# Moving the SBUF buffers of a two-block transformer kernel so that weights and inputs lie 320 bytes apart modulo 512

## The chip, the cores and the metric

The kernel runs on one core of a Trainium2 chip, as one program. The metric is the device time of one execution in microseconds (us). Three runs of the kernel before took 2302.91 to 2307.69 us, with a median of 2307.36 us.

## What is computed

The reference is two blocks of two layers each, on 256 tokens of width 1024, in float32. A layer of the first block is: half a SwiGLU feed-forward of hidden width 2816, an attention mixer (a projection to 2840 columns, three kinds of sparse attention in 8 heads and a further 8 heads of block attention, an output product), and another half feed-forward. A layer of the second block is: a projection, an RWKV-7 recurrence in matrix form, a retention branch and a gated spatial branch, whose results are multiplied by branch weights, weighed by gates and sent through an output product; then a feed-forward of width 2816 with a convolution of three taps.

```
x = x + 0.5 * swiglu(rms_norm(x, norm_ffn1[l]), w_ffn1_gate[l], w_ffn1_up[l], w_ffn1_down[l])
x = x + hybrid_mixer(rms_norm(x, norm_mix[l]), w_in[l], ...)
x = x + 0.5 * swiglu(rms_norm(x, norm_ffn2[l]), ...)
...
x = x + jnp.sum(gates * proj, axis=2) @ w_out[l]
x = x + conv_ffn(rmsnorm(x, norm2_g[l]), ffn_w_up[l], ffn_conv_w[l], ffn_conv_b[l], ffn_w_down[l])
```

## The kernel before

Every large matrix product is made three times, to come near float32 with a faster type: each operand is split into a high and a low part, and `matmul3` (L85 to L91) issues high by high (L89), high by low (L90) and low by high (L91) into the same PSUM bank. Each of the three loads its own 128x128 stationary operand. Weights arrive in SBUF by DMA from the SP queue, ScalarE writes the high part (L341, L351, L638, L1779), VectorE the low part (L417, L435, L645, L1784).

The tokens stand transposed in `hT` (high and low part, 8 blocks of 128 rows by 256 tokens), written once in each phase from four PSUM banks.

**Feed-forward** (`ffn_phase`, four times in the first block, and with `conv` twice in the second). The hidden width is cut into 11 chunks. For chunk i, `hidden(i, slot)` makes the gate and the up product: 2 halves, 2 matrices, 8 blocks, 3 products, so 96 products with a weight block stationary and 256 columns of `hT` moving. Then `down` makes 24 products of the chunk before, with the activation stationary and 512 columns of the down weights moving. Weights of even chunks stand in slot 0 and those of odd chunks in slot 1; the two slots are separate buffers (`mem.parts[slot]`). Chunks 0, 1 and 2 are written out, chunks 3 to 8 are a loop, 9 and 10 are written out again. PE's order is hidden(0), hidden(1), down(0), hidden(2), down(1), hidden(3), down(2) and so on; down uses the slot of its own chunk.

**Mixer and projection** (`nsa_phase`, `rw_project_phase`). Units of 256 weight columns pass through a ring of three buffers. Most jobs are 24 products with weights stationary and 256 columns of `hT` moving; some are turned round, with tokens stationary and 256 (in one unit 280) columns of weights moving. In the mixer, most jobs run in halves of 12 products between steps of the attention.

**Scan and mix** (`scan_mix_phase`). Pieces of 1024 weight columns pass through another ring of three. A gate piece is 24 products with `normed_T_parts` moving, a branch piece 24 with `branches_T` or `rw_T_parts` moving, and an output piece has `merged_parts` stationary and 512 columns of weights moving. Pieces stand between the small products of the recurrence on PE.

At the start of a phase PE turns the normalised tokens, and `keep_clock` (L148) issues products of the identity with itself so that PE doesn't stand still.

All buffers are put at addresses by hand. `first_map` and `second_map` give each a column (4 bytes) from the map's base: the first map holds the buffers of the first block, the second those of the second block. Buffers of different times share memory. The order of work on the engines, the semaphores and the DMA queues do not depend on these columns.

Of the kernel before, what the change touches and what calls it, by code (L numbers as in the profile page):

```python
# [12 lines left out]
P = 128  # L13
D = 1024
KT = D // P
S = 256
# [7 lines left out]
DH = 64  # L24
# [4 lines left out]
Q_COLS = NH * DH  # L29
# [5 lines left out]
CMP_LEN, CMP_STRIDE, CMP_HID = 32, 16, 256  # L35
N_CMP = (S - CMP_LEN) // CMP_STRIDE + 1
CJ = CMP_LEN * DH // P
# [39 lines left out]
F32R = mybir.dt.float32r  # L77
# [164 lines left out]
def blocks(first, *shape):  # L242

    width = KT * FF_W
    if not shape:
        return first
    step = width * int(np.prod(shape[1:]))
    return [blocks(first + n * step, *shape[1:]) for n in range(shape[0])]
# [366 lines left out]
UNIT = KT * 2 * P  # L615
# [49 lines left out]
N_WORK = 3 * NT * 4 * NH + 3 * NT * P + NT * NH  # L665
W_UNIT = KT * (2 * P + GATE_COLS)


def first_map(nc, c):

    def at(name, col, shape, dtype=F32):
        return nc.alloc_sbuf_tensor_at(name, shape, dtype, offset=FIRST_BASE + 4 * col)

    c.ffn = FfnMemory(at, "ffn", dict(hT=0, act=4096, arrived_down=6144, arrived=(blocks(9168, 2), blocks(23152, 2)),
                                      parts=(blocks(13264, 2, 2), blocks(27248, 2, 2)), down_parts=blocks(35440, 2, 2)))
    c.hT_parts = at("mixer_T_parts", 0, [P, 2, KT, S], F32R)
    c.wc1 = at("w_cmp1", 4096, [P, 2, CJ, CMP_HID])
    c.attention = at("attention", 4096, [P, 10 * S + N_WORK])
    c.branch_rows = at("branch_rows", 4096 + 10 * S + N_WORK, [P, 3, Q_COLS])
    c.wc2 = at("w_cmp2", 12288, [P, 2, 2, 2, DH])  # L680
    c.pos = at("pos", 12800, [P, 2, CJ])
    c.raw = at("raw", 12832, [P, N_TURNED, S])
    c.rot = at("rot", 17440, [P, N_ROT, S])
    c.vtok = at("v_tokens", 21024, [P, NT, 2 * P + Q_COLS])
    c.gates = at("gates", 22560, [P, NT, GATE_COLS])
    c.kc = at("k_cmp", 22608, [P, GROUPS, 16])
    c.vc = at("v_cmp_by_head", 22640, [P, NH, DH])
    widths = (UNIT, UNIT, W_UNIT)
    c.units_arrived = [at(f"mixer_arrived{n}", col, [P, w]) for n, (col, w) in enumerate(zip((23152, 25200, 43632), widths))]
    c.units_parts = [[at(f"mixer_parts{n}_{lo}", col + lo * w, [P, w], F32R)[:] for lo in range(2)] for n, (col, w) in enumerate(zip((27248, 31344, 35440), widths))]  # L690
    c.cos_part = c.work[:, 0:2 * S].rearrange("p (a n) -> p a n", a=2)

    c.kcols = c.h[:].rearrange("p t d -> p (t d)")[:, 0:2 * GROUPS * CJ * N_CMP].rearrange(
        "p (v g j n) -> p v g j n", v=2, g=GROUPS, j=CJ)
    hid_w = 2 * 2 * GROUPS * 16
    c.hid = c.work[:, 2 * S:2 * S + hid_w].rearrange("p (v f g n) -> p v f g n", v=2, f=2, g=GROUPS)
    c.hid_v = c.work[:, 2 * S + hid_w:2 * S + hid_w + 2 * NH * 16].rearrange("p (f g r n) -> p f g r n", f=2, g=GROUPS, r=REP)
# [796 lines left out]
def first_block(nc, c, c2, a, start, tables2, out):  # L1494
# [8 lines left out]
    def follow(before, ph):  # L1503
        before.nxt, ph.prev = ph, before

    first_map(nc, c)
    ffn1 = ffn(0, "ffn1")
    ffn1.start = start
# [13 lines left out]
    follow(nsa2, ffn4)  # L1522
    ffn4.count_first()
    second_map(nc, c2)
    halves = [HalfUnits(c2, c2.half_sems, l) for l in range(DEPTH)]

# [127 lines left out]
UNITS = 2 * NH  # L1654
# [44 lines left out]
def second_map(nc, c):  # L1699

    def at(name, col, shape, dtype=F32):
        return nc.alloc_sbuf_tensor_at(name, shape, dtype, offset=SECOND_BASE + 4 * col)

    c.hT_parts = at("normed_T_parts", 0, [P, 2, KT, S], F32R)
    c.vecs = at("vectors", 4096, [P, 40])
    c.mu, c.w0, c.a0, c.k_k, c.k_a, c.r_k = (c.vecs[:, a:b] for a, b in
                                             ((0, 14), (14, 18), (18, 22), (22, 26), (26, 30), (30, 34)))
    c.low_rank = at("low_rank", 4136, [P, 2 * RW_W])
    c.vt = at("rw_v_tokens", 5160, [P, NT, RW_W])
    c.ret_rot = at("ret_rot", 6184, [P, 4, S])  # L1710
    c.ret_v = at("ret_v", 7208, [P, NT, RET_H * RET_V])
    c.ret_g = at("ret_g", 8232, [P, NT, RET_H * RET_V])
    c.st = at("row_stats", 9256, [P, 64])
    kept = at("rw_kept", 9320, [P, 4, PAIRS * S])
    c.gt = at("rw_g_tokens", 13416, [P, NT, RW_W])
    c.bonus = at("rw_bonus", 14440, [P, NT, NH])
    c.rw_small = at("rw_small", 14456, [P, 3, PAIRS, NT])

    LOCAL = 14480
    local = at("rw_local", LOCAL, [P, 8, PAIRS * S])  # L1720
    c.rw = [local[:, n] for n in range(6)] + [kept[:, n] for n in range(4)] + [local[:, n] for n in (6, 7)]
    c.kr = kept[:, 2:4].rearrange("p a n -> p (a n)").rearrange("p (j c n) -> p j c n", j=PAIRS, c=NT)
    c.ret_raw = at("ret_raw", LOCAL + 8192, [P, 4, S])
    c.thin = at("thin", LOCAL + 9224, [P, 2, S])
    c.units_arrived = [at(f"rw_project_arrived{n}", col, [P, UNIT])[:] for n, col in enumerate((36504, 38552, 40600))]
    c.units_parts = [[at(f"rw_project_parts{n}_{lo}", col, [P, UNIT], F32R)[:] for lo, col in enumerate(cols)]
                     for n, cols in enumerate(((24216, 26264), (28312, 34456), (30360, 32408)))]

    c.first_arrived = [at(f"first_project_arrived{n}", col, [P, UNIT])[:] for n, col in enumerate((28312, 40600, 36504))]
    c.first_parts = [[at(f"first_project_parts{n}_{lo}", col, [P, UNIT], F32R)[:] for lo, col in enumerate(cols)]  # L1730
                     for n, cols in enumerate(((24216, 26264), (38552, 34456), (30360, 32408)))]

    c.pairs_of = at("pairs", LOCAL, [P, UNITS, 3 * P])[:]
    c.z_t = at("inverse_T", LOCAL + 6144, [P, UNITS, P])[:]
    c.inner = at("inner", LOCAL + 8192, [P, 2, 512])
    c.rhs0 = at("rw_rhs", LOCAL + 9216, [P, RW_W])
    c.z = at("inverse", 37528, [P, UNITS, P])[:]
    c.low = at("level_rows", 39576, [P, 2, 512])
    c.a_rows = at("a_rows", 34456, [P, UNITS, P])[:]
    c.y_parts = at("branches_T", 26264, [P, 2, 2, 4, S], F32R)  # L1740
    c.half_arrived = [at(f"mix_arrived{n}", col, [P, HALF_UNIT])[:] for n, col in enumerate((40600, 41624, 36504))]
    c.half_parts = [at(f"mix_parts{n}", col, [P, 2, HALF_UNIT], F32R) for n, col in enumerate((30360, 32408, 24216))]
    c.y_rw_parts = at("rw_T_parts", 7208, [P, 2, 4, S], F32R)
    c.merged_parts = at("merged_parts", LOCAL, [P, 2, KT, S], F32R)
    c.conv_ffn = FfnMemory(at, "conv_ffn", dict(hT=18576, act=40600, arrived=(blocks(8192, 2), blocks(26264, 2)), arrived_down=12288,
                                                parts=(blocks(0, 2, 2), ((36504, 38552), (24216, 34456))),
                                                down_parts=((14480, 16528), (30360, 32408)), taps=22672))


R_, K_, V_, A_, LW, KK, BH, KH, KR, KR2, E1, E2 = range(12)  # L1750
# [390 lines left out]
HALF_UNIT = D  # L2141
# [856 lines left out]
```

## Time and profile before

| | |
|---|---|
| median of 3 runs | 2307.36 us |
| the profiled execution | 2309.51 us, its span 2307.7 us |
| PE busy | 2216.4 us, 96% of the span |
| VectorE, ScalarE busy | 1411.9 us, 1005.6 us |
| mean granted clock | 0.981 |
| DMA | 349.08 MB, 41.6% of 16 engines' time |

The profile records the start and a modelled end of each matmul. Matmuls are pipelined, so the duration of one (279 ns for those of 256 columns in the feed-forward) is longer than the step from one start to the next. What a product costs in a row of products is that step: the length of a stretch by the number of products that start in it. In the view of windows, a stretch that begins with the first product of a row and ends with the start of what follows shows its length in the first figure; the count behind it also holds the one to three products of before and after that reach over its edges.

### The profile page before, as it was taken

Reading aid. Unit: us, or ns where it says so; the run is one execution under the profiler, and the core shown is the slowest. Engines: PE = TensorE matmul, PEld = TensorE weight load, DVE = VectorE, ACT = ScalarE, POOL = GpSimd, SP = SyncE. Lnnn points to the kernel's source line nnn. Section 1 sums busy time; section 2 is a strip of 40 time slices with the busy share of each in tenths; the row PEclk is TensorE's granted clock in tenths of the full one; section 3 lists DMA queues with packets and bytes.
Section 4 is the critical chain, followed back from the end, with each engine's and each line's share of the span. In section 5 each row is a group of like instructions: output and inputs, shape, how many; then the busy total and the mean of one; then the engine's idle time right before and its main releaser. Section 6 shows DMA issues by size and latency. Waiting matters only on the chain. (4 is left out here: it accounts for less than half of the span.)

```text
span 2307.7 us, 39093 instructions
## 1 busy us (share of the span) xinstructions
PE 2216.4 (96%) x16210; PEld 2062.3 (89%) x16210; DVE 1411.9 (61%) x2091; ACT 1005.6 (44%) x1409; POOL 18.8 (1%) x18
## 2 busy tenths in 40 slices
PE   7999999999999999999999899899999989989998
PEld 7999977999999997899889799889988979988997
DVE  6545456654654645655476666577677666657775
ACT  5434355433533445633355333364545433336453
POOL 0000000000000000000000100000000010000000
PEclk9999999999999999999999899999999989999999
DMA  8445322553454522354443233365434322336551
GB/s 317 176 157 196 119 101 92 219 216 148 193 214 159 198 84 83 146 219 165 171 148 119 65 96 95 93 254 196 179 114 160 119 76 85 101 96 252 201 182 46
DMA packets 79579, 349.08 MB, mean 151 GB/s; under 512 B 21200, under 2 KB 30544, under 8 KB 45520
## 3 DMA queue, kind: packets, MB, share of 16 engines
q1 hardware_dynamic: 79440, 347.07, 41.6%
q8 instruction: 106, 1.74, 0.3%
q14 instruction: 33, 0.27, 0.0%
HBM read 345.99 MB, written 1.05 MB: 150 GB/s over the span
## 5 line engine op out<-in xcount | busy, mean ns | idle before, releaser
L89 PE MATMUL bank<-ffn_hT_split,n_split_gate_up 128*128 128x256 f32 x1408 | 392.3, 279 | 2.8 <-DVE ffn_hT_split L192 2.7
L90 PE MATMUL bank<-ffn_hT_split,n_split_gate_up 128*128 128x256 f32 x1408 | 392.2, 279 | 0.0
L91 PE MATMUL bank<-ffn_hT_split,n_split_gate_up 128*128 128x256 f32 x1408 | 391.7, 278 | 0.0
L89 PEld LDWEIGHTS bank<-ffn_hT_split,n_split_gate_up 128*128 128x128 f32 x1408 | 265.2, 188 | 4.8 <-issue 3.1
L90 PEld LDWEIGHTS bank<-ffn_hT_split,n_split_gate_up 128*128 128x128 f32 x1408 | 265.1, 188 | 1.5
L91 PEld LDWEIGHTS bank<-ffn_hT_split,n_split_gate_up 128*128 128x128 f32 x1408 | 265.1, 188 | 0.0
L1784 DVE TENSOR_TENSOR mix_parts<-mix_arrived,mix_parts 128x1024 fp32r<-128x1024 f32 x88 | 107.4, 1224 | 137.4 <-ACT mix_parts L1779 137.1
L356 ACT ACTIVATE work<-bank 128x256 f32<-128x256 f32 x88 | 33.3, 383 | 315.6 <-PE bank L91 315.5
L454 DVE TENSOR_TENSOR work<-bank,work 128x256 f32<-128x256 f32 x88 | 37.3, 423 | 197.7 <-ACT work L356 197.7
L435 DVE TENSOR_TENSOR ffn_split_down<-ffn_arrived_down,ffn_split_down 128x2048 fp32r<-128x2048 f32 x44 | 100.8, 2291 | 85.4 <-ACT ffn_split_down L351 85.4
L417 DVE TENSOR_TENSOR n_split_gate_up<-arrived_gate_up,n_split_gate_up 128x2048 fp32r<-128x2048 f32 x64 | 144.7, 2288 | 12.7 <-ACT n_split_gate_up L341 12.7
L1779 ACT ACTIVATE mix_parts<-mix_arrived 128x1024 fp32r<-128x1024 f32 x88 | 92.8, 1056 | 131.5 <-PE bank L91 129.1
L89 PE MATMUL bank<-ffn_split_down,ffn_act_split 128*128 128x512 f32 x352 | 139.0, 395 | 0.0
L91 PE MATMUL bank<-ffn_split_down,ffn_act_split 128*128 128x512 f32 x352 | 138.9, 395 | 0.0
L90 PE MATMUL bank<-ffn_split_down,ffn_act_split 128*128 128x512 f32 x352 | 138.9, 395 | 0.0
L351 ACT ACTIVATE ffn_split_down<-ffn_arrived_down 128x2048 fp32r<-128x2048 f32 x44 | 84.4, 1917 | 112.2 <-PE bank L91 111.6
L341 ACT ACTIVATE n_split_gate_up<-arrived_gate_up 128x2048 fp32r<-128x2048 f32 x64 | 120.1, 1907 | 0.9 <-DMA arrived_gate_up<-in_ffn 0.9
L645 DVE TENSOR_TENSOR mixer_parts<-mixer_arrived,mixer_parts 128x512 fp32r<-128x512 f32 (+2 forms) x74 | 80.1, 1084 | 57.5 <-ACT mixer_parts L638 56.8
L89 PE MATMUL bank<-normed_T_parts,mix_parts 128*128 128x256 f32 x384 | 112.6, 293 | 0.0
L91 PE MATMUL bank<-normed_T_parts,mix_parts 128*128 128x256 f32 x384 | 108.8, 283 | 0.0
L90 PE MATMUL bank<-normed_T_parts,mix_parts 128*128 128x256 f32 x384 | 108.6, 283 | 0.0
L91 PE MATMUL bank<-conv_ffn_hT_split,n_split_gate_up 128*128 128x256 f32 x384 | 107.2, 279 | 0.0
(383 smaller groups left out, 6199.4 us busy)
## 6 DMA issues: line engine op xcount, KB each, us to landing
arrived_gate_up<-in_ffn SPq DMA_DIRECT2D x64, 1024.0 KB, 8.5
ffn_arrived_down<-in_ffn SPq DMA_DIRECT2D x44, 1024.0 KB, 4.9
mix_arrived<-in_mix_w SPq DMA_DIRECT2D x88, 512.0 KB, 3.6
rrived_gate_up<-in_conv_ffn SPq DMA_DIRECT2D x32, 1024.0 KB, 7.1
_arrived_gate_up<-in_ffn SPq DMA_DIRECT2D x24, 1024.0 KB, 6.7
mixer_arrived<-in_w_in SPq DMA_DIRECT2D x22, 1024.0 KB, 6.7
onv_ffn_arrived_down<-in_conv_ffn SPq DMA_DIRECT2D x22, 1024.0 KB, 4.9
irst_project_arrived<-in_w_in SPq DMA_DIRECT2D x17, 1024.0 KB, 4.9
```

The lines of the kernel that those rows point to most:

```text
L89: pe.matmul(out, lhs[0], rhs[0], start=start, stop=False)
L90: pe.matmul(out, lhs[0], rhs[1], start=False, stop=False)
L91: return pe.matmul(out, lhs[1], rhs[0], start=False, stop=stop)
L341: act.activation(flat(w[part][slot][0]), arrived(part, slot), ACT.Copy).then_inc(s["gu_high"], 1)
L351: act.activation(flat(w[2][slot][0]), arrived(2, slot), ACT.Copy).then_inc(s["down_high"], 1)
L356: act.activation(acts[:, slot, f], c.ps[2 * slot + f][:, 0:S], ACT.Silu).then_inc(s["silu_ready"], 1)
L417: dve.tensor_tensor(flat(low), arrived(part, slot), plain(flat(high)), ALU.subtract).then_inc(s["gu_split"], 1)
L435: dve.tensor_tensor(flat(low), arrived(2, slot), plain(flat(high)), ALU.subtract).then_inc(s["down_split"], 1)
L454: dve.tensor_tensor(value, up, value, ALU.mult).then_inc(s["product_ready"], 1)
L645: last = eng.tensor_tensor(self.parts[slot][1][:, cols], self.arrived[slot][:, cols], plain(self.parts[slot][0][:, cols]), ALU.subtract)
L1779: act.activation(self.parts[n % RING][:, 0], self.arrived[n % RING], ACT.Copy).then_inc(self.s["half_high"], 1)
L1784: dve.tensor_tensor(low, self.arrived[n % RING], plain(high), ALU.subtract).then_inc(self.s["half_split"], 1)
```

## The change

Only columns in the two maps change. Distance is used below for the byte address of the stationary operand less that of the moving one, modulo 512. High and low parts, blocks and rows within a buffer lie multiples of 512 bytes apart, but for the third ring buffer of the mixer, whose low part lies 256 bytes further modulo 512. From the columns:

| products | columns moving | distance before | after |
|---|---|---|---|
| feed-forward, hidden, even chunks | 256 | 320 | 320 |
| feed-forward, hidden, odd chunks | 256 | 448 | 320 |
| feed-forward, down | 512 | 64 | 192 |
| mixer, weights stationary | 256 | 448 (low part of the third buffer 192) | 320 (64) |
| mixer, tokens stationary | 256 | 64 | 192 |
| projection, weights stationary | 256 | 96 | 320 |
| projection, tokens stationary | 256 | 416 | 192 |
| gate pieces | 256 | 96 | 320 |
| branch pieces, `branches_T` | 256 | 0 | 0 |
| branch pieces, `rw_T_parts` | 256 | 448 | 160 |
| output pieces | 512 | 480 | 256 |
| convolution feed-forward, hidden, even chunks | 256 | 448 | 320 |
| convolution feed-forward, hidden, odd chunks | 256 | 32 | 320 |
| convolution feed-forward, down, high / low weights | 512 | 32 / 0 | 320 / 0 |

`pos` moves to free memory behind the third arrival buffer, since `w_cmp2` now reaches its old place.

```diff
-    c.ffn = FfnMemory(at, "ffn", dict(hT=0, act=4096, arrived_down=6144, arrived=(blocks(9168, 2), blocks(23152, 2)),
-                                      parts=(blocks(13264, 2, 2), blocks(27248, 2, 2)), down_parts=blocks(35440, 2, 2)))
-    c.hT_parts = at("mixer_T_parts", 0, [P, 2, KT, S], F32R)
-    c.wc1 = at("w_cmp1", 4096, [P, 2, CJ, CMP_HID])
-    c.attention = at("attention", 4096, [P, 10 * S + N_WORK])
+    c.ffn = FfnMemory(at, "ffn", dict(hT=32, act=4128, arrived_down=6176, arrived=(blocks(9200, 2), blocks(23152, 2)),
+                                      parts=(blocks(13296, 2, 2), blocks(27248, 2, 2)), down_parts=blocks(35440, 2, 2)))
+    c.hT_parts = at("mixer_T_parts", 32, [P, 2, KT, S], F32R)
+    c.wc1 = at("w_cmp1", 4128, [P, 2, CJ, CMP_HID])
+    c.attention = at("attention", 4128, [P, 10 * S + N_WORK])
...
-    c.pos = at("pos", 12800, [P, 2, CJ])
+    c.pos = at("pos", 43632 + W_UNIT, [P, 2, CJ])
...
-    c.units_arrived = [at(f"rw_project_arrived{n}", col, [P, UNIT])[:] for n, col in enumerate((36504, 38552, 40600))]
+    c.units_arrived = [at(f"rw_project_arrived{n}", col, [P, UNIT])[:] for n, col in enumerate((36560, 38608, 40656))]
-                     for n, cols in enumerate(((24216, 26264), (28312, 34456), (30360, 32408)))]
+                     for n, cols in enumerate(((24272, 26320), (28368, 34512), (30416, 32464)))]
...
-    c.y_parts = at("branches_T", 26264, [P, 2, 2, 4, S], F32R)
-    c.half_arrived = [at(f"mix_arrived{n}", col, [P, HALF_UNIT])[:] for n, col in enumerate((40600, 41624, 36504))]
-    c.half_parts = [at(f"mix_parts{n}", col, [P, 2, HALF_UNIT], F32R) for n, col in enumerate((30360, 32408, 24216))]
+    c.y_parts = at("branches_T", 26320, [P, 2, 2, 4, S], F32R)
+    c.half_arrived = [at(f"mix_arrived{n}", col, [P, HALF_UNIT])[:] for n, col in enumerate((40656, 41680, 36560))]
+    c.half_parts = [at(f"mix_parts{n}", col, [P, 2, HALF_UNIT], F32R) for n, col in enumerate((30416, 32464, 24272))]
...
-    c.conv_ffn = FfnMemory(at, "conv_ffn", dict(hT=18576, act=40600, arrived=(blocks(8192, 2), blocks(26264, 2)), arrived_down=12288,
-                                                parts=(blocks(0, 2, 2), ((36504, 38552), (24216, 34456))),
-                                                down_parts=((14480, 16528), (30360, 32408)), taps=22672))
+    c.conv_ffn = FfnMemory(at, "conv_ffn", dict(hT=18560, act=40656, arrived=(blocks(8272, 2), blocks(26320, 2)), arrived_down=12368,
+                                                parts=(blocks(80, 2, 2), ((36560, 38608), (24272, 34512))),
+                                                down_parts=((14464, 16512), (30416, 32464)), taps=22672))
```

## Rows read from the trace of the kernel before

**Rows 1.** The page: busy time of engines, and granted clock in 40 slices.

```profile
PE 2216.4 (96%) x16210; PEld 2062.3 (89%) x16210; DVE 1411.9 (61%) x2091; ACT 1005.6 (44%) x1409; POOL 18.8 (1%) x18
...
PEclk9999999999999999999999899999999989999999
```

**Rows 2.** Windows of two stages: length, busy time and count by engine, clock, DMA.

```profile
395.00:573.00 178.00, 178.00 (x1296) 167.04 (x1295) 98.29 (x100) 70.87 (x58) 0.00 (x0) 1.00 0.48 186
...
1540.00:1720.00 180.00, 180.00 (x1284) 168.75 (x1283) 130.20 (x187) 86.93 (x100) 0.00 (x0) 1.00 0.46 167
```

**Rows 3.** Windows, PE alone: five chunks of hidden products and one of down.

```profile
29.16:40.04 10.88, 10.88 (x99) 1.00 0.79 290
45.63:56.52 10.89, 10.89 (x98) 1.00 0.66 257
62.11:73.42 11.31, 11.31 (x98) 1.00 0.50 188
...
394.64:405.83 11.19, 11.19 (x98) 1.00 0.17 44
405.83:417.13 11.30, 11.30 (x98) 1.00 0.66 255
...
73.42:79.01 5.59, 5.59 (x26) 1.00 0.45 185
```

**Rows 4.** Timeline of PE at the start of the second feed-forward.

```profile
393.74 0.94 PE L148 MATMUL bank<-shared_tables 128*128 128x128 f32 x7
394.44 0.36 PE L89 MATMUL bank<-ffn_hT_split,n_split_gate_up 128*128 128x256 f32 x1
```

**Rows 5.** Windows, PE alone, of the other families of products.

```profile
1565.60:1576.91 11.31, 11.31 (x98) 1.00 0.48 182
1548.64:1560.00 11.36, 11.36 (x98) 1.00 0.80 310
1560.00:1565.60 5.60, 5.60 (x27) 1.00 0.57 199
1479.64:1482.37 2.73, 2.73 (x25) 1.00 0.00 0
2053.99:2056.69 2.70, 2.70 (x26) 1.00 0.00 0
209.86:221.17 11.31, 11.31 (x99) 1.00 0.87 309
1165.58:1171.28 5.70, 5.70 (x50) 1.00 0.70 253
1495.27:1500.93 5.66, 5.66 (x51) 1.00 0.31 88
1818.83:1824.59 5.76, 5.76 (x51) 1.00 0.52 182
322.83:323.97 1.14, 1.14 (x11) 1.00 0.95 402
```

**Rows 6.** Groups of instructions by line and form: L90, one of three alike lines.

```profile
L90 PE MATMUL bank<-ffn_hT_split,n_split_gate_up 128*128 128x256 f32 x1408 | 392.2, 279 | 0.0
...
L90 PE MATMUL bank<-normed_T_parts,mix_parts 128*128 128x256 f32 x384 | 108.6, 283 | 0.0
...
L90 PE MATMUL bank<-mixer_T_parts,mixer_parts 128*128 128x256 f32 x288 | 81.7, 284 | 0.0
...
L90 PE MATMUL bank<-normed_T_parts,rw_project_parts 128*128 128x256 f32 x144 | 41.6, 289 | 0.0
...
L90 PE MATMUL bank<-rw_project_parts,normed_T_parts 128*128 128x256 f32 x128 | 36.2, 283 | 0.0
...
L90 PE MATMUL bank<-rw_T_parts,mix_parts 128*128 128x256 f32 x64 | 19.6, 306 | 0.0
...
L90 PE MATMUL bank<-mixer_parts,mixer_T_parts 128*128 128x256 f32 x64 | 17.8, 277 | 0.0
```

**Rows 7.** Waits of PE over the span: total, times, longest.

```profile
PE bank L89 <- DVE rw_local L1949: 7.0, 5, 3.0
```

More of the change, by code:

```diff
@@ L672, in at @@
         return nc.alloc_sbuf_tensor_at(name, shape, dtype, offset=FIRST_BASE + 4 * col)
-    c.ffn = FfnMemory(at, "ffn", dict(hT=0, act=4096, arrived_down=6144, arrived=(blocks(9168, 2), blocks(23152, 2)),
-                                      parts=(blocks(13264, 2, 2), blocks(27248, 2, 2)), down_parts=blocks(35440, 2, 2)))
-    c.hT_parts = at("mixer_T_parts", 0, [P, 2, KT, S], F32R)
-    c.wc1 = at("w_cmp1", 4096, [P, 2, CJ, CMP_HID])
-    c.attention = at("attention", 4096, [P, 10 * S + N_WORK])
-    c.branch_rows = at("branch_rows", 4096 + 10 * S + N_WORK, [P, 3, Q_COLS])
-    c.wc2 = at("w_cmp2", 12288, [P, 2, 2, 2, DH])
-    c.pos = at("pos", 12800, [P, 2, CJ])
+    c.ffn = FfnMemory(at, "ffn", dict(hT=32, act=4128, arrived_down=6176, arrived=(blocks(9200, 2), blocks(23152, 2)),
[3 more added lines that the diff above has]
+    c.attention = at("attention", 4128, [P, 10 * S + N_WORK])
+    c.branch_rows = at("branch_rows", 4128 + 10 * S + N_WORK, [P, 3, Q_COLS])
+    c.wc2 = at("w_cmp2", 12320, [P, 2, 2, 2, DH])
+    c.pos = at("pos", 43632 + W_UNIT, [P, 2, CJ])
     c.raw = at("raw", 12832, [P, N_TURNED, S])
@@ L1724, in second_map @@
     c.thin = at("thin", LOCAL + 9224, [P, 2, S])
-    c.units_arrived = [at(f"rw_project_arrived{n}", col, [P, UNIT])[:] for n, col in enumerate((36504, 38552, 40600))]
+    c.units_arrived = [at(f"rw_project_arrived{n}", col, [P, UNIT])[:] for n, col in enumerate((36560, 38608, 40656))]
     c.units_parts = [[at(f"rw_project_parts{n}_{lo}", col, [P, UNIT], F32R)[:] for lo, col in enumerate(cols)]
-                     for n, cols in enumerate(((24216, 26264), (28312, 34456), (30360, 32408)))]
-    c.first_arrived = [at(f"first_project_arrived{n}", col, [P, UNIT])[:] for n, col in enumerate((28312, 40600, 36504))]
+                     for n, cols in enumerate(((24272, 26320), (28368, 34512), (30416, 32464)))]
+    c.first_arrived = [at(f"first_project_arrived{n}", col, [P, UNIT])[:] for n, col in enumerate((28368, 40656, 36560))]
     c.first_parts = [[at(f"first_project_parts{n}_{lo}", col, [P, UNIT], F32R)[:] for lo, col in enumerate(cols)]
-                     for n, cols in enumerate(((24216, 26264), (38552, 34456), (30360, 32408)))]
+                     for n, cols in enumerate(((24272, 26320), (38608, 34512), (30416, 32464)))]
     c.pairs_of = at("pairs", LOCAL, [P, UNITS, 3 * P])[:]
@@ L1736, in second_map @@
     c.rhs0 = at("rw_rhs", LOCAL + 9216, [P, RW_W])
-    c.z = at("inverse", 37528, [P, UNITS, P])[:]
-    c.low = at("level_rows", 39576, [P, 2, 512])
-    c.a_rows = at("a_rows", 34456, [P, UNITS, P])[:]
-    c.y_parts = at("branches_T", 26264, [P, 2, 2, 4, S], F32R)
-    c.half_arrived = [at(f"mix_arrived{n}", col, [P, HALF_UNIT])[:] for n, col in enumerate((40600, 41624, 36504))]
-    c.half_parts = [at(f"mix_parts{n}", col, [P, 2, HALF_UNIT], F32R) for n, col in enumerate((30360, 32408, 24216))]
+    c.z = at("inverse", 37584, [P, UNITS, P])[:]
+    c.low = at("level_rows", 39632, [P, 2, 512])
+    c.a_rows = at("a_rows", 34512, [P, UNITS, P])[:]
+    c.y_parts = at("branches_T", 26320, [P, 2, 2, 4, S], F32R)
+    c.half_arrived = [at(f"mix_arrived{n}", col, [P, HALF_UNIT])[:] for n, col in enumerate((40656, 41680, 36560))]
+    c.half_parts = [at(f"mix_parts{n}", col, [P, 2, HALF_UNIT], F32R) for n, col in enumerate((30416, 32464, 24272))]
     c.y_rw_parts = at("rw_T_parts", 7208, [P, 2, 4, S], F32R)
     c.merged_parts = at("merged_parts", LOCAL, [P, 2, KT, S], F32R)
-    c.conv_ffn = FfnMemory(at, "conv_ffn", dict(hT=18576, act=40600, arrived=(blocks(8192, 2), blocks(26264, 2)), arrived_down=12288,
-                                                parts=(blocks(0, 2, 2), ((36504, 38552), (24216, 34456))),
-                                                down_parts=((14480, 16528), (30360, 32408)), taps=22672))
+    c.conv_ffn = FfnMemory(at, "conv_ffn", dict(hT=18560, act=40656, arrived=(blocks(8272, 2), blocks(26320, 2)), arrived_down=12368,
+                                                parts=(blocks(80, 2, 2), ((36560, 38608), (24272, 34512))),
+                                                down_parts=((14464, 16512), (30416, 32464)), taps=22672))
 R_, K_, V_, A_, LW, KK, BH, KH, KR, KR2, E1, E2 = range(12)
```

## The prediction

> **What bounds the kernel now.** I read the page's busy shares first: PE is busy 96% of the span, with a clock near full in all 40 slices [rows 1]. The windows by stage say the same more sharply: in the second feed-forward PE is busy 178.00 of 178.00 us and in the convolution feed-forward 180.00 of 180.00, VectorE 98 and 130 us [rows 2]. So the end is set by how fast PE steps from product to product, and a change that alters nothing but that step passes to the span nearly whole. That is why I went on to windows cut at the first product of a row, and divided by 96 (chunks), 24 (down) and so on.
>
> They show two steps for the same work. The 96 hidden products of chunk 3 of the first feed-forward (odd, distance 448) take 11.31 us, 117.8 ns each; chunk 2 (even, 320) takes 10.89, 113.4 ns [rows 3]. Instructions, shapes and granted clock (1.00) are equal. DMA is not the cause: the last 95 products of chunk 0 of the second feed-forward take 11.19 us (117.8 ns) at a DMA share of 0.17, chunk 1 of the first takes 10.88 at 0.79 [rows 3]. What differs is the place of the weights, or what the row began with.
>
> These last two windows also speak against distance alone. Chunk 1 of the first feed-forward has distance 448 and is fast: it follows chunk 0 without a break. Chunk 0 of the second has 320 and is slow: it follows identity products [rows 4], and chunk 1 behind it takes 11.30 [rows 3]. So there are two paces, a row keeps the one it has, and something at its beginning chooses.
>
> Other families, as ns per step from the windows of [rows 5], in the order of the rows: convolution chunk 2 (distance 448) 11.31/96 = 117.8; its chunk 1 (32) 11.36/96 = 118.3; convolution down 5.60/24 = 233.3; gates (96) 2.73/23 = 118.7 and 2.70/23 = 117.4; mixer (448) 11.31/96 = 117.8; projection (96) 5.70/48 = 118.8; `rw_T` pieces (448) 5.66/48 = 117.9; projection with tokens stationary (416) 5.76/48 = 120.0; mixer with tokens stationary (64) 1.14/10 = 114.0. The fast pace stands at 320 and 64, the others at 117 to 120. The two fast ones are 256 apart.
>
> **The change part by part.** No instruction, wait or DMA is added, removed or reordered. I value each family at its step before less 113.4, where its distance becomes 320.
>
> 1. Feed-forward, odd chunks (448 to 320). In each of four phases chunks 3, 5, 7 and 9 follow a row of down products, as the fast even chunks do: 16 x (11.31 - 10.89) = 16 x 0.42 = 6.7 us [rows 3]. For chunks 0 and 1 of phases 2 to 4 I count nothing, since chunk 0 is slow at 320 already; chunk 1 of the first is fast.
> 2. Convolution feed-forward. Chunks 2 to 10 follow down products. Even ones 11.31 - 10.89 = 0.42, odd ones 11.36 - 10.89 = 0.47 [rows 3, 5]: 5 x 0.42 + 4 x 0.47 = 3.98 a layer, 8.0 in two. Chunks 0 and 1, behind identity products, count nothing.
> 3. Gates: 3 x 384 products [rows 6], mean of the two steps 118.0, so 1152 x 4.6 ns = 5.3 us. They begin behind small products, not down products. That such a beginning allows the fast pace is shown by the mixer's tokens-stationary rows at 64, which begin so.
> 4. Projection, weights stationary: 144 for each of two buffer names and three lines, 864 products [rows 6], six of 18 jobs in each layer behind identity products. The other 576 x (118.8 - 113.4) = 3.1 us.
> 5. Mixer, weights stationary: 3 x 288 = 864 [rows 6], likewise without the first six jobs of 24 in each layer: 576 x (117.8 - 113.4) = 2.5 us.
> 6. Tokens stationary, distance 192 in the changed kernel. No row has 192. In the projection 768 products take 120.0 (128 x 3 for each of two names) [rows 5, 6]; the ends are 114.0, the fastest row of this form, which gains 4.6 us, and 120.0, no gain. As 320 and 64 behave alike 256 apart, I take 192 to behave like 448: 117.9, a gain of 1.6. In the mixer 192 products go from 114.0 to the same 117.9: a loss of 0.7; ends 0 and a loss of 1.2 at 120.0 [rows 5].
> 7. `rw_T` pieces, 448 to 160: 192 products at 117.9 [rows 5, 6]; ends 113.4 (a gain of 0.9) and 120.0 (a loss of 0.4). I take the loss, since 160 lies 256 from the slow 416.
> 8. Down and output products, 512 columns: feed-forward down at distance 64 takes 5.59/24 = 232.9 [rows 3], convolution down at 32 and 0 takes 233.3 [rows 5]. The distance doesn't show; I take nothing. With the 1584 down products half a nanosecond either way is 0.8 us.
> 9. The moved `pos`, the shifted arrival buffers, and the splits on ScalarE and VectorE: nothing. They are covered by PE, which is full beside 98 to 130 us of VectorE in 180 [rows 2]; if that cover went, the splits would be late for the products, and the rows of waits would name a split.
>
> Sum: 6.7 + 8.0 + 5.3 + 3.1 + 2.5 + 1.6 - 0.7 - 0.4 = 26.1 us. PE waits 7.0 us in five places for VectorE's mixing in the projection [rows 7], and a shorter job only lengthens such a wait: I take off 1.1, a third of part 4. That leaves 25.0. The profiled execution took 2309.5, so 2284.5; the median of the runs lies 2.1 lower, which gives 2307.4 - 25.0 = 2282.4, rounded to 2282.
>
> **The rivals.**
>
> *The row's beginning chooses, and the change takes the good one away (slower).* The first weight load of a chunk runs beside the last down product. Counted from that product's moving weights, the first load of even chunks lies at 384 before and of odd chunks at 0; in the changed kernel both lie at 0. If 0 is what makes a row slow, the 20 fast even chunks that follow down products become slow: 20 x 0.42 = 8.4 us [rows 3], and with parts 6 and 7 at their bad ends (1.2 + 0.4) and nothing gained elsewhere 2307.4 + 10 = 2317. It decides the sign once about half of those chunks turn and the convolution and the gates gain nothing. For it: pace is plainly inherited, and slow at 320 behind identity products. Against it: all other families at 0, 32, 96, 416 and 448 are slow behind every kind of beginning, the tokens-stationary rows at 64 fast, and a first load alone doesn't explain that.
>
> *Distance isn't the cause.* What the two slots differ in may be the buffer, not the distance: then odd chunks stay slow, nothing else moves, 2307. For it: chunk 1 fast at 448 and chunk 0 slow at 320 [rows 3]. Against it: chunk 2 and chunk 0 share a buffer and differ in pace.
>
> The Trainium skill (page SBUF — State Buffer, section Who interferes with whom) says that PE and ACT never wait on anyone, and its page TensorE: Matmul & The Clock Gate (section Step-by-step: what each phase is for) that the weights and the moving operand have two independent read ports, so that loading the next weights takes no read bandwidth from the running matmul. By that rule no distance matters and the time stays at 2307. The two paces of equal products in [rows 3] do not fit it.
>
> *Only rows behind down products gain.* Parts 1 and 2 hold, gates, projection and mixer keep their pace: 14.7 less the 1.1 of parts 6 and 7 (with no gain in 6), so 2307.4 - 13.6 = 2294.
>
> *All rows gain.* Those behind identity products too: six chunks of 0.42 in the first block, four of about 0.45 in the second, 288 products x 4.4 ns and 288 x 5.4 ns: 2.5 + 1.8 + 1.3 + 1.6 = 7.2 more, 2275.
>
> **How the numbers follow.** My forecast 0.50, only behind down products 0.14, all rows 0.10, no cause 0.14, slower 0.12. The likeliest gives 2282; its own range, by the ends of parts 6 to 8 and half of parts 3 to 5, is 2277 to 2291. The range that should hold 8 in 10 runs from 2273, just under the case of all rows, to 2310, just over no change; most of the slower case is left out. A change of 0.2%, 4.6 us, is about what a measurement can tell from none. Faster by more: the first three cases, less a little for a gain eaten elsewhere, 0.71; within it: no cause, and a weak slower case, 0.15; slower 0.14.
>
> **What would show it.** Windows from the first hidden product of chunks 3, 5, 7, 9 to the next down: 10.9 us if part 1 holds, 11.3 if not; chunks 2, 4 and on at 11.3 would be the slower rival. Convolution chunks likewise. A gate's 23 steps at 2.61 instead of 2.73 show part 3, 24 projection steps at 2.72 part 4. Projection rows with tokens stationary at 5.66 per 48 show part 6; 5.76 or more its bad end. Chunks 0 and 1 of the second feed-forward at 10.9 show that all rows gain. I am wrong if PE's step is unchanged where the distance became 320, or if it shrinks and new waits of PE appear by as much.

## The result and the profile after

Six runs of the changed kernel have a median of 2288.3 us (2286.85 to 2296.8), six of the kernel before, taken with them, 2307.53 (2302.91 to 2313.78). The ratio is 0.9924, with a 95% interval of 0.9903 to 0.9944: faster by 0.8%, 6 us above the 2282 forecast and inside its range. Two of the twelve runs of the first map alone, and two of the 23 of the kernel before beside them, were over 1% longer at a lower granted clock; ratios leave them out. The profiled execution took 2289.41 us with a span of 2287.6, 20.1 less than the span before.

The page after, in the lines that answer to [rows 1]:

```profile
PE 2191.7 (96%) x16210; PEld 2043.6 (89%) x16210; DVE 1411.2 (62%) x2091; ACT 1005.3 (44%) x1409; POOL 18.8 (1%) x18
...
PEclk9999999999999999999999899999999989999999
```

PE has the same 16210 products and is busy 24.7 us less, VectorE 0.7 and ScalarE 0.3. The time came from PE's step, but about 3 us of it only by where the granted clock was low, as the sums below show. The span fell by 20.1, so 4.6 of the 24.7 came back as idle PE. The waits of PE over the span say where: the largest one, of a phase's first transposes (L162) for VectorE's norm, was this in the kernel before,

```profile
PE bank L162 <- DVE normed L141: 23.4, 13, 10.2
```

and is this after (columns: total us, times, longest):

```profile
PE bank L162 <- DVE normed L141: 28.5, 15, 11.0
```

It accounts for 5.1. The norm's instructions take VectorE as long as before (748 and 749 ns each), but their wait is not one thing. The longest, at the start of the program, grew by 0.8, before any product that was moved. At the start of the second and the fourth feed-forward it grew by 0.9 each: before, the 18 identity products there ran at a granted clock of 0.50 and took 3.69 and 3.80 us, with no wait behind them; after, they ran at 1.00, took 2.17, and left a wait of 0.8. At the start of the second convolution feed-forward it grew by 1.6.

The windows of the kernel after, PE alone (length, busy time and count, clock, DMA share, GB/s), are those on which the steps of the prediction are judged:

```profile
30.31:41.62 11.31, 11.31 (x98) 1.00 0.78 285
47.22:58.12 10.90, 10.90 (x97) 1.00 0.61 238
63.62:74.52 10.90, 10.90 (x97) 1.00 0.47 178
391.87:402.65 10.78, 10.78 (x97) 1.00 0.17 46
402.65:413.53 10.88, 10.88 (x99) 1.00 0.66 258
58.12:63.62 5.50, 5.50 (x27) 1.00 0.52 216
1532.40:1543.70 11.30, 11.30 (x98) 1.00 0.80 315
1549.30:1560.62 11.32, 11.32 (x98) 1.00 0.53 193
1543.70:1549.30 5.60, 5.60 (x26) 1.00 0.52 177
2103.14:2114.02 10.88, 10.88 (x98) 1.00 0.86 338
1327.37:1329.87 2.50, 2.50 (x24) 1.00 0.65 185
1332.78:1335.37 2.59, 2.59 (x24) 1.00 0.62 179
1462.77:1465.38 2.61, 2.61 (x26) 1.00 0.00 0
1167.30:1169.90 2.60, 2.60 (x25) 1.00 0.89 337
1175.93:1178.64 2.71, 2.71 (x25) 1.00 0.83 311
231.12:233.62 2.50, 2.50 (x24) 1.00 1.03 424
237.86:240.57 2.71, 2.71 (x25) 1.00 0.33 79
1800.31:1805.96 5.65, 5.65 (x50) 1.00 0.53 186
323.06:324.00 0.94, 0.94 (x10) 1.00 0.99 261
1481.82:1484.70 2.88, 2.88 (x26) 1.00 0.66 182
1490.31:1493.03 2.72, 2.72 (x13) 1.00 0.55 160
```

Rows 1 to 6 are the first feed-forward's chunks 1, 2 and 3, the second's chunk 0 (its last 95 products) and chunk 1, and a row of down products; they answer to [rows 3]. Even and odd chunks behind down products take 10.90 us, the odd one 0.41 less than before. The second phase's chunks 0 and 1 are fast now, the first phase's chunk 1 slow. Down takes 5.50 instead of 5.59.

Rows 7 to 10 are the convolution feed-forward: chunks 1 and 2 and down of its first layer, then chunk 1 of its second. At distance 320, 11.30 and 11.32: nothing of the forecast 0.42 to 0.47 came but 0.05 on the odd chunks; only layer 2's chunks 0 and 1, for which nothing was forecast, became fast.

The others are: two gates behind the same kind of product (22 steps of 113.6 and of 117.7 ns), a third (23 of 113.5); the projection with weights stationary, 23 steps of 113.0 in one job and of 117.8 in another; the mixer likewise, 22 of 113.6 and 23 of 117.8; tokens stationary in the projection, 48 of 117.7, and in the mixer 8 of 117.5; 24 `rw_T` products of 120; and 12 output products of 226.7 ns. All but the last answer to [rows 5].

To see each family's share I added, in both traces, the steps from every product's start to the next within a job. The two traces also differ in where the granted clock stood at 0.50, the lower of its two levels: there a product of 256 columns takes 213 to 214 ns and one of 512 columns 426 to 427. In the kernel before this fell on about 157 of these products, after on 130. Two such stretches of the kernel before, in a mixer job and in an output piece:

```profile
239.20:242.00 2.80, 2.80 (x15) 0.50 0.88 313
2095.91:2098.89 2.98, 2.98 (x8) 0.50 1.02 431
```

The last column is the part of the gain that is only this, each slow product less the step of its job at full clock. The sums are of unrounded values.

| part of the prediction | products | gain forecast, us | gain in the steps, us | of it by the low clock, us |
|---|---|---|---|---|
| 1 | feed-forward, hidden | 6.7 | 7.8 | 0.1 |
| 2 | convolution, hidden | 8.0 | 1.4 | 0 |
| 3 | gates | 5.3 | 3.4 | 0.5 |
| 4 | projection, weights stationary | 3.1 | 2.4 | 0.7 |
| 5 | mixer, weights stationary | 2.5 | 2.5 | 1.2 |
| 6 | projection and mixer, tokens stationary | 0.9 | 1.0 | 0 |
| 7 | `rw_T` pieces | -0.4 | -1.1 | -0.8 |
| 8 | feed-forward down; convolution down; output | 0 | 4.4; -0.5; 2.4 | 0; 0; 1.4 |
| none | mixer's output products | - | 0.3 | 0 |
| | sum | 26.1 | 24.0 | 3.0 |

The sum is nearly right, its terms are not; without the low clock it is 21.1. What the low clock made in the medians is not known, since one execution of each kernel was traced. The mixer's 192 output products of 512 columns went from distance 64 to 192 like its other products with tokens stationary; the table of the change and the prediction leave them out.

### The profile page after: what moved, and what is told of

Same layout as the page of the kernel before. It is cut to its first block and busy times, and to the rows that moved or that the text cites. A ratio compares the mean times of both kernels' runs of the same rounds, so it can differ in the third digit from the quotient of the medians.

```text
span 2287.6 us, 39093 instructions
## 1 busy us (share of the span) xinstructions
PE 2191.7 (96%) x16210; PEld 2043.6 (89%) x16210; DVE 1411.2 (62%) x2091; ACT 1005.3 (44%) x1409; POOL 18.8 (1%) x18
## 5 line engine op out<-in xcount | busy, mean ns | idle before, releaser
L90 PE MATMUL bank<-ffn_hT_split,n_split_gate_up 128*128 128x256 f32 x1408 | 390.0, 277 | 0.0
L90 PEld LDWEIGHTS bank<-ffn_hT_split,n_split_gate_up 128*128 128x128 f32 x1408 | 265.2, 188 | 1.5
L90 PE MATMUL bank<-ffn_split_down,ffn_act_split 128*128 128x512 f32 x352 | 138.0, 392 | 0.0
L90 PE MATMUL bank<-normed_T_parts,mix_parts 128*128 128x256 f32 x384 | 107.7, 281 | 0.0
```

Source lines behind the costliest of these rows:

```text
L90: pe.matmul(out, lhs[0], rhs[1], start=False, stop=False)
```

## The experiments

Three theories had to be told apart. A: a product's own distance sets its pace. B: the pace is taken over from what stands ahead of the row, the down products above all. C: the buffer or slot matters, not the distance. Each kernel below does all of the work.

**Even chunks to 448, odd ones left at 320** (from the changed kernel).

```diff
-  parts=(blocks(13296, 2, 2), blocks(27248, 2, 2))
+  parts=(blocks(13328, 2, 2), blocks(27248, 2, 2))
```

> The changed kernel, with the even chunks' weights of the first block's feed-forward moved on by 128 bytes: even chunks at distance 448, odd chunks left at 320, everything else as it is. Theory A (the distance of a row's own operands sets its pace): even chunks from chunk 2 on take 11.3 us per 96 products, odd ones stay at 10.9; 20 slow chunks more, so some 8.4 us over the changed kernel. Theory B (what the row begins with decides, the distance of its own operands does not): even and odd chunks stay alike, 10.9 each. Theory C (the buffer decides): the slow ones would be the odd chunks.

One run, 2302.34 us. Windows of chunks 2, 3 and 4 and of the down products behind 2 and behind 3:

```profile
46.41:57.71 11.30, 11.30 (x98) 1.00 0.63 244
63.31:74.21 10.90, 10.90 (x98) 1.00 0.48 178
79.71:91.01 11.30, 11.30 (x97) 1.00 0.50 185
57.71:63.31 5.60, 5.60 (x27) 1.00 0.44 183
74.21:79.71 5.50, 5.50 (x27) 1.00 0.53 222
```

Slow and fast have changed slots with the distance, so C falls. The down products, whose addresses are those of the changed kernel, take 5.60 behind a slow chunk and 5.50 behind a fast one: pace can be handed on from chunk to down as well.

**Only the feed-forward's down products from 64 to 192** (from the kernel before).

```diff
-  dict(hT=0, act=4096, arrived_down=6144,
+  dict(hT=0, act=4128, arrived_down=6176,
```

> The kernel before, with the activation of the first block's feed-forward moved on by 128 bytes: the down products at distance 192 instead of 64, the hidden products left at 320 (even) and 448 (odd). If the 512-column products have a pace of their own distance, 24 of them take 5.49 us as in the changed kernel instead of 5.59: 44 chunks x 0.1 = 4.6 us less in all. Theory A: odd chunks stay at 11.3 us. Theory B, with the state that the down products leave behind: odd chunks become 10.9, a further 6.7 us less.

One run, 2302.31 us. Windows of chunk 1, down, chunk 2, down, chunk 3, down, chunks 4 and 5:

```profile
30.74:41.63 10.89, 10.89 (x99) 1.00 0.67 257
41.63:47.13 5.50, 5.50 (x27) 1.00 0.97 396
47.13:58.44 11.31, 11.31 (x97) 1.00 0.69 263
58.44:64.04 5.60, 5.60 (x27) 1.00 0.45 190
64.04:75.35 11.31, 11.31 (x98) 1.00 0.50 193
75.35:80.85 5.50, 5.50 (x26) 1.00 0.43 179
80.85:91.75 10.90, 10.90 (x98) 1.00 0.47 174
97.24:108.55 11.31, 11.31 (x97) 1.00 0.50 191
```

The 512-column products have a pace of their own distance: 5.50 at 192 against 5.59 at 64, without any edit of the chunks. The odd chunks, at 448, stay at 11.31, so these down products don't cure them, and the down row behind slow chunk 3 is fast: a slow chunk doesn't always slow the down row behind it. Chunk 2, at 320, is slow in the first three phases, and the down row behind it takes 5.60; the even chunks from 4 on are fast. In the fourth phase chunk 2 is fast as well. There chunk 1, at 448, is slow, while in the first three it is fast. Chunks 1 and 2 of the fourth phase:

```profile
968.51:979.81 11.30, 11.30 (x99) 1.00 0.65 254
985.32:996.22 10.90, 10.90 (x98) 1.00 0.64 241
```

The down row between them takes 5.51, against 5.50 in the first phase. So the same operands behind the same down products came out with both paces, and the chunk ahead of the down row went with it: in this kernel a chunk at 320 was slow behind a fast chunk at 448, and fast behind a slow one. Neither A nor B explains this.

**First map alone, second map alone.** Each is the kernel before with the lines of the diff that belong to one map.

> The kernel before with the first map of the changed kernel, so only the first block's addresses change. In the traces the second block starts 12.9 us earlier after the change. If that is the first map's doing alone, this kernel gains 13 us, ratio 0.994; the theory of my forecast (odd chunks 6.7, mixer 1.8) would give 8.5, ratio 0.996. Feed-forward chunks from 2 on 10.9 us whether even or odd, down 5.49.

> The kernel before with the second map of the changed kernel. The traces leave 7.2 us of the 20.1 to the second block: ratio 0.997. My forecast for this half was 16.5 us (convolution 8.0, gates 5.3, projection 3.6, the rw_T pieces against it), ratio 0.993. Convolution chunks at 11.3 us, down at 5.6.

Twelve and ten runs: the first map's median is 2300.17 us, ratio 0.9961 (0.9946 to 0.9976); the second's 2302.33, ratio 0.9975 (0.9960 to 0.9990). Their product is 0.9936, the change as a whole 0.9924: the two halves add up within the intervals, and the second, for which the prediction had counted more, brings less by the medians, though the intervals of the two overlap.

**The convolution feed-forward with all distances of the plain one** (from the changed kernel): down goes from 320/0 to 192, the chunks stay where they are.

```diff
-  dict(hT=18560, act=40656,
+  dict(hT=18560, act=40704,
...
-  down_parts=((14464, 16512), (30416, 32464))
+  down_parts=((14416, 16464), (30416, 32464))
```

> The changed kernel, with the convolution feed-forward's activation and high down weights moved so that all its operands have the distances of the first block's feed-forward: hidden 320 (as it is), down 192 instead of 320 and 0, first hidden load 0 from the last down weights instead of 320. Theory A with its own distances: hidden chunks stay at 11.3 us (they are at 320 already), the down products go from 5.60 to 5.49 us per 24: 22 x 0.11 = 2.4 us less than the changed kernel. Theory B (the down products before a row choose between the two paces that 320 allows): chunks 2 to 10 go to 10.9 as well, 18 x 0.42 = 7.6 us more, some 10 us less than the changed kernel in all, ratio to the kernel before about 0.988.

Five runs, median 2281.46 us (2275.87 to 2285.07), ratio to the kernel before 0.9876 (0.9855 to 0.9897). Windows of chunks 1, 2 and 3, of down, and of 24 `rw_T` products:

```profile
1529.87:1540.75 10.88, 10.88 (x98) 1.00 0.81 316
1546.25:1557.15 10.90, 10.90 (x97) 1.00 0.71 271
1562.64:1573.55 10.91, 10.91 (x97) 1.00 0.43 157
1540.75:1546.25 5.50, 5.50 (x27) 1.00 0.40 125
1479.18:1482.06 2.88, 2.88 (x26) 1.00 0.62 188
```

No weight and no input of a hidden chunk was moved, and every chunk behind down products went from 11.31 to 10.90. That is B. This version beats both kernels: the page's PE busy time is 2180.2 us, 11.5 less than after the change.

**Only the convolution's down weights moved**, the activation left: down at 0/0.

```diff
-  down_parts=((14464, 16512), (30416, 32464))
+  down_parts=((14416, 16464), (30416, 32464))
```

> The changed kernel, with only the high down weights of the convolution feed-forward moved: the first hidden load lies 0 from the last down weights instead of 320, as in the first block's feed-forward, but the down products themselves are at distance 0 instead of 320 and 0. If the first load against the last down weights decides, hidden chunks take 10.9 us; if the down products' own distance decides, they stay at 11.3. Theory A: 11.3.

One run, 2287.45 us. Windows of chunks 1 and 3 and of a down row:

```profile
1533.17:1544.47 11.30, 11.30 (x98) 1.00 0.84 328
1566.68:1577.99 11.31, 11.31 (x98) 1.00 0.38 138
1544.47:1549.93 5.46, 5.46 (x26) 1.00 0.45 162
```

The down weights, and with them the place of a chunk's first weight load against the moving down weights, are those of the version before this one; only the distance to the activation differs. Down at 0 is faster by itself (the later rows take 226.7 ns a product, against 228.9 at 192), and the chunks behind it stay slow. So neither the first load alone nor the speed of the row ahead is what a chunk takes over; the place of the row's activation is, and the reading that fits is its distance to the down weights. The same edit also changes the activation's distance to the chunk's input, from 0 in the version before to 320 here.

**Crossed** (from the changed kernel): the feed-forward's down at 0, the convolution's at 0 for the high and 192 for the low weights.

```diff
-  dict(hT=32, act=4128, arrived_down=6176,
+  dict(hT=32, act=4208, arrived_down=6256,
...
-  dict(hT=18560, act=40656,
+  dict(hT=18560, act=40704,
```

> The changed kernel with two activations moved. In the first block's feed-forward the activation goes to distance 0 from the down weights, which is what the convolution feed-forward had when only its down weights were moved. Theory B (the distance of the down products chooses the pace of the row behind them): 24 down products go from 5.49 to 5.44 us, and the hidden chunks from 2 on, at 320 as before, fall to 11.3, 36 chunks x 0.42 = 15 us more; theory A: they stay at 10.9. In the convolution feed-forward the activation alone moves: down at 0 (high weights) and 192 (low weights), the first hidden load 320 from the last down weights. If one row of down products at a good distance is not enough, chunks stay at 11.3.

One run, 2302.03 us. Windows of the feed-forward's chunk 1, chunks 2 and 3 and down, then the convolution's chunk 1, down and a later chunk:

```profile
30.25:41.13 10.88, 10.88 (x98) 1.00 0.74 291
46.59:57.89 11.30, 11.30 (x97) 1.00 0.69 272
63.33:74.64 11.31, 11.31 (x98) 1.00 0.50 193
57.89:63.33 5.44, 5.44 (x26) 1.00 0.44 182
1543.08:1554.39 11.31, 11.31 (x98) 1.00 0.78 305
1571.28:1576.84 5.56, 5.56 (x26) 1.00 0.80 305
1576.84:1588.15 11.31, 11.31 (x97) 1.00 0.36 131
```

The fault has been made in the feed-forward: chunk 1, ahead of any down products, is fast; chunks 2 and 3, behind down at 0, are slow, at the 320 that is fast in the changed kernel. Down at 0 saves 0.06 us a row against 192 and costs the next chunk 0.41. The convolution's chunks stay slow with the activation at 0 from their input, as with the cure, so that distance alone does not decide either. But there, as in the changed kernel's convolution, the first load lies at 320 from the last down weights, not at 0; for these two kernels the part at 0 and the first load are not told apart.

**The convolution's cure, and `rw_T` from 160 to 320.**

```diff
-  c.y_rw_parts = at("rw_T_parts", 7208, [P, 2, 4, S], F32R)
+  c.y_rw_parts = at("rw_T_parts", 7168, [P, 2, 4, S], F32R)
```

> The changed kernel with the convolution feed-forward at the distances of the other one (the best run so far), and the rw_T parts moved by 160 bytes, so that their products go from distance 160 to 320. Theory A: 192 products at 119.6 ns go to 113.4 or stay at 117.7 by how they begin, 0.4 to 1.2 us less; that is under what the timing can tell, so the trace decides. Ratio to the kernel before 0.987 to 0.988.

Six runs, median 2286.76 us (2275.0 to 2299.36), ratio 0.9910 (0.9877 to 0.9944). Two `rw_T` pieces, 48 products:

```profile
1487.88:1493.32 5.44, 5.44 (x51) 1.00 0.59 175
```

That is 113.3 ns a product, where the kernel without this edit has 2.88/24 = 120.0: another family that is fast at 320. The runs spread over 24 us, partly with the mean granted clock (2275.0 at 0.985, 2294.75 at 0.977, 2299.36 at 0.980), so the time can't show a gain of one microsecond, and I don't rank this version against the one with the convolution's cure alone.

## Why the prediction was nearly right in the sum and wrong in its terms

The bound was right. PE's step sets the end, VectorE and ScalarE kept their times, and PE's busy time fell by 24.7 us where the terms ahead of the waits gave 26.1. That it came so near is luck: without the low clock the steps gave 21.1, the low clock gave another 3.0 that was not forecast, and the errors of the terms went both ways. The waits took 4.6 instead of the 1.1 taken off, and mostly at another place: the norm at the start of phases, not the projection's mixing, whose five waits went from 7.0 to 7.2 us [rows 7].

**Part 1 held.** The odd chunks went from 11.31 to 10.90, as in "16 x 0.42". The extra microsecond comes with chunks 0 and 1 of phases 2 to 4, which became fast, less those of the first phase, which became slow. In the four other traces with the feed-forward's addresses of the changed kernel the chunks 0 and 1 came out otherwise (phase 1 slow in the changed kernel and fast in the four; phase 3 slow in one of the five), while chunks 2 and on were the same in all five. With the addresses of before it is the same: in the kernel with the second map alone the chunks 0 and 1 of phases 2 to 4 are fast, where they were slow in the kernel before. A row behind identity products starts with either pace, so the execution and not the map decides the rival "all rows gain" here, and the extra microsecond is luck too.

**Part 2 failed, and it is the step that cost the forecast most**: 8.0 us forecast, 1.4 found. Its words "Chunks 2 to 10 follow down products" treated being behind down products as enough. I had read from [rows 3] that a row keeps the pace it has, and did not ask what pace the down products, which the change moves to 320/0, would hand on. The rows of the experiments answer it for chunks at 320:

| down products' distance | ns a down product | the chunk behind |
|---|---|---|
| 64 (before, feed-forward) | 233 | fast |
| 192 (after; convolution's cure) | 228.9 | fast |
| 0 (crossed; down weights alone) | 226.7 | slow |
| 320/0 (after, convolution) | 234 | slow |
| 0/192 (crossed, convolution) | 232.1 | slow |

The three rows that have a part at 0 are those with 11.31 us behind them; it is the one rule tried that fits all five, and the slow chunk 2 with only down moved, at 192, stands outside it. So the rival about a row's beginning had the mechanism in part: the row ahead does take the good pace away. But it put the cause in the place of the first weight load, and the down-weights experiment excludes that as the only cause: its first load is at 0, as where chunks are fast. The rival also looked in the wrong stage, the first block. An own distance is still needed: in the first experiment 448 is slow behind the same down products as 320 is fast.

**Part 3 was mis-sized.** "That such a beginning allows the fast pace" was right, but it allows the slow one as well: 27 of the 48 gate pieces run at 113 to 114 ns, and 27 x 24 x 4.6 ns = 3.0 us, what is left of the 3.4 found without the low clock's 0.5. Through most of a layer fast and slow alternate, behind the same kind of small product.

**Parts 4 and 5** were mis-sized as well. They seem near their sums, but 0.7 of the 2.4 and 1.2 of the 2.5 are the low clock; without it 1.7 is left for 3.1, and 1.3 for 2.5. The jobs behind the first six are not all fast (the windows show jobs at 113.0 and 117.8 in one projection).

**Part 6 held**, 1.0 for 0.9: 192 behaves like 448, 117.7 where 117.9 was taken. **Part 7 held** without the low clock, -0.3 for -0.4; 160 costs 120.0 instead of 117.9.

**Part 8 failed in the useful direction.** "The distance doesn't show" rested on 64 and 32/0, which agree at 233. The experiment on down alone shows 229 at 192; in the feed-forward that is 4.4 us. The output products went from 233.1 to 226.7 ns as their distance went from 480 to 256, about 1.1 us; the rest of their 2.4 is the low clock. With the convolution's -0.5 and the mixer's 0.3 that is 5.3, which the forecast had at nothing and which by luck made good most of the missing 6.6 of part 2.

The rival "distance isn't the cause" is out by the first experiment, where slow and fast changed slots with the distance. The Trainium skill (page SBUF — State Buffer, section Who interferes with whom) says that PE never waits on anyone, and its table gives PE two read ports that are independent of each other. The traces here differ: the same 96 products behind down products take 10.90 or 11.31 us in kernels that differ in byte addresses alone, and the same 24 down products 5.44, 5.50 or 5.60. What inside the chip makes the difference no run here shows.

What stays open: which event picks the pace of a row behind identity products, why the gates alternate, from a layer's third on, in the same order in every execution with these addresses that I compared, and how, where only down was moved, the pace of chunk 1 came through the down row and turned into its opposite in chunk 2. In the gates of the changed kernel the first step is 200 or 201 ns in 19 of the 20 rows at 117.8 ns, and 202 to 207 in 20 of the 25 rows at 113 to 114, so a difference of a nanosecond or two at the beginning may decide; this was seen, not tested.

## What to carry to other kernels

Where an engine is full and only its step is left to win, compare the step of equal instructions between places in the trace, and before a layout is changed list the distances of all neighbours in the row, not only of the products to be cured: here the neighbours' place decided 6.6 us of 8. Set the stretches at a lower clock apart before a gain in the steps is put down to the change: in this pair of traces they made 3 us of 24. A pace that is inherited must be forecast along the chain, row by row. A term taken as nothing because two rows agree is not a bound; the run with down alone at 192 showed the 4.4 us that it hid.

## What the runs showed of the hardware

- A product of 256 moving columns had two paces in its rows at full clock, 113.3 and 117.7 ns, and another near 120 at distances 160 and 416. At a granted clock of 0.50 it took 213 to 214 ns, one of 512 columns 426 to 427. Rows behind down products were fast at 320 alone and slow at 448; 320 is not enough, since such rows were slow there too.
- A product of 512 columns took 226.7 ns at 0 and 256, 228.9 at 192, 233 at 64 and at 480, and 234 at 320/0; at 192 also 233 behind some slow chunks.
- A pace lasts for a whole row, and can go over into the next one across a change of shape: from chunk to down (5.60 behind a slow chunk, 5.50 behind a fast one, with the same addresses in the first experiment), while from down to chunk the pace of the down row did not go over: chunks were slow behind 5.44 and fast behind 5.60.
- Chunk 1 of the second feed-forward is fast in the changed kernel at a DMA share of 0.66, as its chunk 0 at 0.17: the pace did not follow the transfers.
